# Two attention stages that begin under their last key projection, with z projected beside the values

## The reference, cut to what matters

```python
q, k, v, z = jnp.split(u @ w_in, 4, axis=-1)          # four 1024 x 1024 projections
# differential: 8 pairs of heads, 64 wide; p is the softmax of each half
sc = einsum('bqhmd,bkhmd->bhmqk', qblk, k) + bias
p = softmax(where(dist >= 0, sc, NEG))
a = p[:, :, 0] - lam * p[:, :, 1]
o = rmsnorm(einsum('bhqk,bkhe->bqhe', a, v), subln) * (1 - lambda_init)
y = (o * silu(z)) @ w_out
# grid: 16 heads, 64 wide, each query sees 8 rows x 16 columns of keys
pr = softmax(s + bias)
y = (einsum('bhwij,biwjhd->bwhd', pr, v_win) * silu(z)) @ w_out
```

## Time and profile before

| | |
|---|---|
| median of three runs | 1489.68 us |
| profiled execution, own time / span | 1490.42 / 1488.6 us |
| PE matmul busy | 1391.8 us, 93% |
| DVE, ACT, POOL busy | 42%, 48%, 52% |
| mean granted TensorE clock | 0.980 |
| differential stage: last product of z ends, flow's first score starts | 605.8 us |
| grid stage: the same | 931.0 us |

### The profile page before, as it was taken

How to read it: one execution, slowest core, us unless ns; L and a number is a source line. 1 busy time by engine, 2 the same in 40 slices (tenths; PEclk the granted TensorE clock), 3 DMA queues, 4 the chain that set the end, 5 groups by cost and what they waited for, 6 DMA issues and landing times.

```text
span 1488.6 us, 20916 instructions
## 1 busy us (share of the span) xinstructions
PE 1391.8 (93%) x7818; PEld 1133.3 (76%) x7818; DVE 620.4 (42%) x1602; ACT 712.6 (48%) x1522; POOL 777.5 (52%) x722
## 2 busy tenths in 40 slices
PE   6999999999989999888989999889999999999997
PEld 5877777777878888766778888768878787677785
DVE  3321067787151110596151110781442135888143
ACT  4242258887343223575342333882544244788252
POOL 5362356666445344365554433795646434566652
PEclk9999999999999999799999999899999999999999
DMA  6232310000433222111443232315224222001521
GB/s 235 85 114 85 114 57 30 30 30 1 156 110 145 101 97 87 55 44 43 170 138 117 90 109 85 142 58 212 99 85 184 85 85 85 2 1 41 201 85 57
DMA packets 27876, 139.57 MB, mean 94 GB/s; under 512 B 3328, under 2 KB 3712, under 8 KB 16128
## 3 DMA queue, kind: packets, MB, share of 16 engines
q1 hardware_dynamic: 14112, 98.57, 18.3%
q10 hardware_dynamic: 13664, 39.66, 7.7%
HBM read 129.83 MB, written 8.39 MB: 93 GB/s over the span
## 4 chain that ended last, share of the span: by engine, by line
PE 71%; POOL 10%; DVE 9%; ACT 5%; issue 2%; DMA 1%; ACTq 1%; POOLq 0%; SPq 0%; DVEq 0%
PE psum L379 57%; PE psum L1109 3%; POOL w_free L1249 3%; POOL w_lo L334 3%; PE psum L1092 3%; DVE w_free L1154 2%; PE psum L1068 2%; PE psum L827 2%; DVE u_lo L1167 2%; DMA w_raw<-in_weights 1%; POOL split L1266 1%; ACT w_hi L327 1%; PE psum L1081 1%; DVE arena L700 1%; ACT u_hi L1199 1%
## 5 line engine op out<-in xcount | busy, mean ns | idle before, releaser
L334 POOL TENSOR_TENSOR w_lo<-w_raw,w_hi 128x2048 fp32r<-128x2048 f32 (+1 forms) x111 | 425.5, 3846 | 462.4 <-ACT w_hi L327 462.0
L379 PE MATMUL psum<-u_lo,w_hi 128*128 128x512 f32 (+1 forms) x712 | 279.3, 392 | 4.2 <-DVE split L464 1.6
L379 PE MATMUL psum<-u_hi,w_lo 128*128 128x512 f32 (+1 forms) x712 | 277.6, 390 | 0.0
L379 PE MATMUL psum<-u_hi,w_hi 128*128 128x512 f32 (+1 forms) x712 | 277.6, 390 | 0.0
L327 ACT ACTIVATE w_hi<-w_raw 128x2048 fp32r<-128x2048 f32 x90 | 172.1, 1913 | 150.0 <-DMA w_raw<-in_weights 102.7
L379 PE MATMUL psum<-w_hi,split 128*128 128x512 f32 x608 | 196.0, 396 | 4.5 <-POOL w_lo L334 2.6
L748 ACT ACTIVATE w_free<-w_free,neg_max 128x256 f32<-128x256 f32 (+3 forms) x320 | 183.5, 580 | 6.3 <-DVE neg_max L1154 3.9
L379 PEld LDWEIGHTS psum<-u_lo,w_hi 128*128 128x128 f32 (+1 forms) x712 | 133.6, 188 | 33.7 <-issue 4.0
L379 PEld LDWEIGHTS psum<-u_hi,w_hi 128*128 128x128 f32 (+1 forms) x712 | 133.4, 187 | 28.8
L379 PEld LDWEIGHTS psum<-u_hi,w_lo 128*128 128x128 f32 (+1 forms) x712 | 133.5, 187 | 27.7
L379 PE MATMUL psum<-w_hi,u_lo 128*128 128x512 f32 (+2 forms) x352 | 135.6, 385 | 10.4 <-DVE u_lo L706 7.8
(11 more groups left out here) (188 smaller groups left out, 2190.0 us busy)
## 6 DMA issues: line engine op xcount, KB each, us to landing
w_raw<-in_weights SPq DMA_DIRECT2D x90, 1024.0 KB, 4.8
x<-x_scratch ACTq DMA_DIRECT2D x12, 512.0 KB, 6.5
gain<-in_gains ACTq DMA_DIRECT2D x10, 512.0 KB, 4.4
gain<-in_strips ACTq DMA_DIRECT2D x16, 256.0 KB, 3.0
spare<-in_strips ACTq DMA_DIRECT2D x16, 256.0 KB, 2.9
x_scratch<-x ACTq DMA_DIRECT2D x16, 256.0 KB, 4.1
gain<-in_near ACTq DMA_DIRECT2D x8, 512.0 KB, 4.3
w_raw<-in_near ACTq DMA_DIRECT2D x8, 512.0 KB, 3.8
```

Of the source, the lines that this page charges most:

```text
L334: low = nc.gpsimd.tensor_tensor(w_lo[b][:, c], w_raw[b][:, c], w_hi[b][:, c].bitcast(F32), ALU.subtract)
L379: mm = nc.tensor.matmul(dst, lhs, rhs, start=(a == 0 and k == 0 and (wl, ul) == (0, 1)), stop=(a + 1 == u and k + 1 == nk and (wl, ul) == ...
```

## The change

In the differential and the grid stage alike:

- z is projected right after v, then q, then k.
- Of k, half 0 runs as before. Half 1's first unit (a=0) goes to banks 4 to 7 (`begin_last`). Its second unit (a=1), the last four product groups before the attention, is issued group by group between the flow's first scores (`last_keys`). ACT and DVE take each bank out inside the flow (`last_keys_high`, `last_keys_low`), and PE's first `turn`s and `values` wait until their bank is empty.
- On ACT `high(0)` comes one iteration later than before, after the last of these takes. In the grid stage DVE's `score(4)` moves ahead of the last two takes.
- Unit out+1 can be loaded only once the last key products are done. Its high part is made by ACT in step 10 (differential) or 12 (grid), its low part by POOL in four quarters in steps 11 to 14 or 13 to 16.
- The ring is no longer n mod 3: units out+1 and out+2 change places, by the tables SLOT, BEFORE and NTH, so that `p_map` lies where half 1's first key unit lay.

```diff
+        swapped = [RUNS[name]["unit"] + 1 for name in ("diff_out", "na_out")]
+        for n in range(SLOTS, N_UNITS):
+            BEFORE.append(n - 2 if n in swapped else n - 4 if n - 1 in swapped else n - SLOTS)
+            SLOT.append(SLOT[BEFORE[n]])
...
+        def begin_last(pe, f):
+            run = RUNS[f.last]
+            pe.wait_ge(w_ready, run["unit"] + 3)
+            for j in range(NT):
+                mm = products(pe, run, 1, 0, j, base=4)
+            mm.then_inc(w_used, 1)
+        def last_keys(pe, f, j):
+            run = RUNS[f.last]
+            pe.wait_ge(w_ready, run["unit"] + 4)
+            products(pe, run, 1, 1, j, base=4).then_inc(bank_done, 1)
+        def last_keys_high(act, f, j):
+            act.wait_ge(bank_done, 4 * (RUNS[f.last]["block"] + 1) + j + 1)
+            at_ = KH + (4 + j) * T
+            nc.scalar.activation(split[:, at_:at_ + T], bank(4 + j), ACT.Copy).then_inc(split_hi, 1)
+        def last_keys_low(dve, f, nth, j):
+            dve.wait_ge(split_hi, 4 * (nth + 1) + j + 1)
+            nc.vector.tensor_tensor(split[:, lo_:lo_ + T], bank(4 + j), split[:, hi_:hi_ + T].bitcast(F32), ALU.subtract)
...
@@ diff_tensor
                 if i < f.steps:
                     scores(i)
+                if i < NT:
+                    last_keys(pe, f, i)
                 if 0 <= i - LAG < f.steps:
                     turn(i - LAG)
@@ diff_vector
                     combine(i - 3)
+                if 1 <= i <= NT:
+                    last_keys_low(dve, f, 8, i - 1)
@@ diff_scalar
+                if 1 <= i <= NT:
+                    last_keys_high(act, f, i - 1)
+                if i == NT:
+                    high(0)
+                if i == 10:
+                    split_high(act, RUNS["diff_out"]["unit"] + 1)
@@ diff_pool
+                if 11 <= i < 15:
+                    split_low(pool, RUNS["diff_out"]["unit"] + 1, i - 11)
@@ pair_tensor
+                if f.last and i < LAG + 1:
+                    for j in ((0,), (1,), (2, 3))[(i + 1) // 2]:
+                        last_keys(pe, f, j)
@@ pair_vector
+                if f.last and i == LAG + 1:
+                    score(i)
+                if f.last and 1 <= i <= LAG + 1:
+                    for j in ((0,), (), (1,), (2, 3))[i - 1]:
+                        last_keys_low(dve, f, 14, j)
@@ pair_scalar
+                if f is na_flow and i == 12:
+                    split_high(act, RUNS["na_out"]["unit"] + 1)
@@ pair_pool
+                if f is na_flow and 13 <= i < 17:
+                    split_low(pool, RUNS["na_out"]["unit"] + 1, i - 13)
@@ tensor
-            for name in ("diff_q", "diff_k", "diff_z"):
+            for name in ("diff_z", "diff_q"):
                 project_tensor(pe, name)
+            project_tensor(pe, "diff_k", only=(0,))
+            begin_last(pe, diff_flow)
             begin(pe, diff_flow)
             diff_tensor(pe, diff_flow)
```

More of the change, by code:

```diff
@@ L238, in p_map @@
             s = i % 4
[L239 removed]
+            home = w_free[SLOT[RUNS[f.name + "_out"]["unit"] + 2]]
             if f is na_flow:
@@ L308, in _ @@
             for n in range(SLOTS, N_UNITS):
-                used, count = consumed(n - SLOTS)
+                used, count = consumed(BEFORE[n])
                 sp.wait_ge(used, count)
@@ L350, in _program, with products @@
         WIDE_FROM = {"ple0_proj": (PHI, PLO), "ple1_proj": (PHI, PLO), "mla_k": (LATENT_HI, LATENT_LO), "mla_v": (LATENT_HI, LATENT_LO)}
-        def products(pe, run, i, a, j, banks=4, gated_by=None, between=None):
+        def products(pe, run, i, a, j, banks=4, gated_by=None, between=None, base=0):
             w, nk, u = run["width"], run["nks"][a], len(run["nks"])
@@ L735, in begin @@
             run = RUNS[f.name + "_out"]
-            eng.wait_ge(bank_free["dve"], 4 + run["taken"])
+            eng.wait_ge(bank_free["dve"], 4 + run["taken"] - (4 if f.last else 0))
             eng.wait_ge(bank_free["act"], 4 + run["others"])
@@ L1185, in pair_vector @@
                     inverse(i - 2)
-                if i < f.steps:
+                if i < f.steps and not (f.last and i == LAG + 1):
                     score(i)
```

88 lines of the change are left out of this document (56 added, 32 removed).

## The result

The changed kernel takes 1496.35 us, the median of 20 runs (1487.75 to 1503.54), against 1489.35 us for the kernel before in as many (1480.33 to 1500.12). The ratio is 1.0043, with a 95% interval of 1.0025 to 1.0062: it is slower by about 6.4 us. The profiled execution took 1496.65 us, 6.23 more than that of before. The forecast was 1491.2 with a range to 1495.5; the median lies outside it.

The account below looks back on a forecast made before the run. PE was busy 93% of the span, but at full clock DVE bound the differential flow and POOL the grid flow. Differential +2.4 - 1.0 and grid +0.9 - 3.9 made it 1.6 us slower: 1491.2 us, range 1483.5 to 1495.5.

Parts of the forecast that it names:

- Differential start: Start of the differential flow: score(4) at t+15.65 in place of t+18.1, a lead of 2.4 us.
- t: Start of the last four product groups before the attention: 594.90 us for the differential flow, 920.14 for the grid flow.
- The first fall: Differential flow, behind the last product: PE's clock falls to 1.2 GHz again, six in ten, price 5.8 us.
- Out+1 in the differential flow: ACT's high part and POOL's four quarters in the differential steps: cost taken as 1.0 us together.
- Grid start: Start of the grid flow: score(5) at t+18.2 in place of t+19.1, a lead of 0.9 us.
- Out+1 in the grid flow: Grid flow: POOL is the bound, four quarters cost 5.1 us, 1.2 taken back from idle time: 3.9.
- I take 0: Grid flow: ACT's 1.91 us for out+1 falls beside POOL's quarters, cost 0 to 1.9 us, taken as 0.
- What costs nothing: Both stages: z earlier, out+1's load, the grid bias and spilled x cost nothing; a failure costs about 5 us.
- Sum: Whole kernel: differential +2.4 - 1.0, grid +0.9 - 3.9, so 1.6 us slower, 1491.2 us.
- Rival C: Grid flow pays out+1's full price, 7.1 us slower; differential flow 1.4 faster; 1495.4 us, chance 0.21.
- B: Differential flow keeps 2.4 GHz, grid flow doesn't: +8.2 - 1.0 - 3.0, 4.2 us faster, 1485.5 us, chance 0.31.

Follow-up runs that it names:

- e2: Changed kernel, differential out+1 split earlier: ACT's high part in iteration 7, POOL's quarters in 8 to 11, behind root_heads and split_heads; ratio 0.9996 to the kernel before.
- e9: Kernel before with the differential stage alone changed, out+1 split early, PE making scores(5) two more times in its wait; 1481.59 us, ratio 0.9931.
- e1: Changed kernel, POOL's differential quarters kept in iterations 11 to 14 but put behind root_heads and split_heads; ratio 1.003 to the kernel before.
- e3: Changed kernel, differential out+1 split late: high part on ACT in iteration 33, low part whole on POOL in 34; 1495.62 us, ratio 1.0015.
- e13: Changed kernel, PE making differential scores(19) three more times, filling its 2.35 us wait; ratio 1.0029 to the kernel before.
- e11: Changed kernel with the early differential split; in the grid flow only ACT's high part moved, from iteration 12 to 6; ratio 1.0031 to the kernel before.
- e7: e2 with PE making differential scores(5) two more times in its wait behind the last product; 1487.61 us, ratio 0.9975 to the kernel before.
- e10: e2 with the grid split early too: ACT's high part in iteration 5, POOL's quarters in 6 to 9; ratio 0.9991 to the kernel before.
- e15: e9 measured again, unchanged; 1479.07 us, ratio 0.9925 to the kernel before.
- e12: Kernel before, PE making differential scores(3) two more times in its 1.99 us wait; ratio 0.9995 to the kernel before.

## Why the prediction was wrong, step by step

- **Differential start, lead 2.4 forecast.** At `score(11)` 4.1, of which 0.5 were there at the fall near 424 us already. Of the other 3.6: t was set 1.0 too late (594.9 less 0.5, against 593.40), because 605.78 held the 0.78 us wait that the changed kernel does not have; `score(4)` then came 16.3 after that start instead of 15.65 (the text's 0.96 is 0.88 by its own rows, 1.36 less 0.48, so that isn't the reason); and the slow stretch was 20.5 instead of 23.9 us (0.9). PE's 1.40 us of waiting was exact.
- **The first fall comes back, six in ten, 5.8 us.** It came back in every profile of the interleaved kernels whose wait was not filled, and was worth 5.8 us when it went (e2 to e9). The row that the text called agreement with the rule, PE 98% busy at 0.50 for 23.9 us, doesn't bear it out: there PE was active and the clock was not released.
- **Out+1 in the differential flow, taken at 1.0 with 0 to 5.0 as its ends: this is the step that failed.** It cost 7.3 us, more than its upper end. The text said that POOL's "own time is hidden" since it idles 16 of 50 us, and asked only whether DVE would be held. The order on POOL, which it left out, made half of the direct loss: `root_heads`, for which ACT waits, stood behind the quarter (e1). Idle time of an engine in sum is no slack for the instruction next in its queue. These waits and DVE's holds together made 3.0 us (e3, e13). The other 4.1 were no price of an engine at all: PE starved, and the clock fell for 13.7 us in a flow that had kept it. The rule of the Trainium skill that the prediction weighed ("SBUF — State Buffer", "SBUF: two separate sides") points at a real hold, 0.5 us of `ratio` and 0.65 of `combine` above; its share of the 3.0 us isn't measured by itself, and all four quarters, with their holds, cost 0.5 us in e2.
- **Grid start, lead 0.9 forecast.** 2.2 measured: again t contained a wait of 0.84 us (922.21 against 920.14 + 3.2: 1.1 too late), and the slow stretch was 3.4 us in place of 10.2 (1.1). Against it `score(5)` came 19.2 after that start instead of 18.2. The 2.6 us of waiting was exact (2.59). That the earlier trace rows gives 0.35 for a `score` is misread, it shows 0.42; 0.34 is what lies between the starts of two.
- **Out+1 in the grid flow, 3.9 forecast.** 5.2, the price of the quarters (5.1) in full: the 1.2 us that POOL was to win back from its idle time were not won. ACT's "I take 0" held, since e11's quarters without it lost 5.4 in the same stretch.
- **What costs nothing** held: z alone is 0.9999.
- **Sum.** -0.5 - 3.6 + 7.3 - 2.2 + 5.2 = 6.2 us, the difference of the two profiled executions. Rival C was on the right side and had nothing won back in the grid flow, which is right. But its other terms are wrong: the quarters ran at 1.27 us and not above 1.4, ACT's 1.9 did not come on top, and it put no loss in the differential flow. That its 1495.4 lies near the measured 1496.35 is luck. B's gain of 8.2 there was to be had, but by e9's filling and not by the change.

What stays open: what makes the same instructions fall or keep the clock (e7 and e9; e2 and e10), how long the second fall is in executions that were not profiled, and why the runs of e9 and e15 stay within 1475.6 to 1483.7 us while those of e12 spread from 1483.3 to 1500.3. The first fall, too, isn't fixed: in e10's profile, with the same start as e2, it lasted 34.1 us.

## What to carry to other kernels

When an operation is put into a pipeline, look for what stands directly behind it in that engine's queue and who waits for that, since a mean idle share says nothing of it: three iterations earlier and behind the operation that is waited for, the same work cost 0.5 us instead of 7.1, and behind it alone 4.0. On an engine that is the bound, place does not help and only the amount counts. And where PE waits (1.4 and 2.35 us here), the clock that falls behind it can cost more (5.8 and 4.1 us) than the wait itself. Where PE's next inputs lie ready, repeating that work in the wait is a cheap thing to try first; try it in more than one execution, since it kept the clock in three profiles of the same stage and not in the fourth. A flow that got faster in its profile isn't yet a faster kernel (e3).
